# Low parts of the normed input on GpSimd instead of VectorE, in seven of the kernel's normalisations

## What is computed

```
def rms_norm(x, g):
    y = x * rsqrt(mean(x * x, axis=-1) + 1e-6)
    return y * g
...
u = rms_norm(h, norm_mix_g[l]);  h = h + mixer_sublayer(u, ...)
h = h + conv_ffn(rms_norm(h, norm_ffn_g[l]), w_up[l], ...)
# conv_ffn: (silu(causal_conv3(h @ w_up's gate half)) * (h @ w_up's value half)) @ w_down
```

## Time and profile before

| | before |
|---|---|
| median of 3 runs | 2057.96 us (2057.04 to 2058.07) |
| the profiled execution's own time | 2058.53 us |
| its span, first to last instruction | 2056.7 us |
| TensorE busy, weight load busy | 2043.4 us, 1925.8 us |
| VectorE busy | 1704.2 us (83%) |
| ScalarE busy | 1104.8 us (54%) |
| GpSimd busy | 289.1 us (14%), 197 instructions |

### The profile page before, as it was taken

The page is one execution under the profiler, slowest core; times in us unless marked ns, Lnnn a source line. Parts: engine busy times, 40 slices in busy tenths (PEclk is TensorE's granted clock), DMA queues, the critical chain, the costliest instruction groups (busy, mean ns, idle before and its releaser), DMA issues.

```text
span 2056.7 us, 35431 instructions
## 1 busy us (share of the span) xinstructions
PE 2043.4 (99%) x14722; PEld 1925.8 (94%) x14722; DVE 1704.2 (83%) x2507; ACT 1104.8 (54%) x1428; POOL 289.1 (14%) x197
## 2 busy tenths in 40 slices
PE   9999999999999999999999999999999999999998
PEld 9999999899999989979989999899988999989897
DVE  8988899888789988898996669777798996758875
ACT  6887366457756635355455445535346445445542
POOL 0212055000004500001201001510000300000430
PEclk9999999999999999999999999999999999999999
DMA  7563555554235465544555444555554554535543
GB/s 267 196 194 142 185 182 185 186 208 144 103 145 183 160 212 198 184 163 148 202 185 185 164 145 184 180 169 208 184 175 150 185 186 183 185 127 182 186 166 119
DMA packets 58287, 361.74 MB, mean 176 GB/s; under 512 B 6736, under 2 KB 9360, under 8 KB 21136
## 3 DMA queue, kind: packets, MB, share of 16 engines
q1 hardware_dynamic: 58128, 359.48, 49.5%
HBM read 358.37 MB, written 1.08 MB: 175 GB/s over the span
## 4 chain that ended last, share of the span: by engine, by line
PE 87%; DVE 7%; issue 2%; ACT 2%; POOL 1%; DMA 0%; SPq 0%; DVEq 0%; ACTq 0%; POOLq 0%
PE acc L651 47%; PE acc L675 11%; PE acc L658 8%; PE acc L650 7%; PE acc L665 4%; DVE w_lo L1226 2%; ACT w_hi L2217 1%; DVE arena L1720 1%; PE acc L795 1%; PE acc L796 1%; PE acc L797 1%; DVE arena L1466 1%; PE acc L1001 1%; DVE arena L1717 1%; PE pA L1050 1%
## 5 line engine op out<-in xcount | busy, mean ns | idle before, releaser
L651 PE MATMUL acc<-in_both,w_hi 128*128 128x256 f32 x6000 | 1092.9, 285 | 1.8 <-issue 0.7
L651 PE MATMUL acc<-in_both,w_lo 128*128 128x256 f32 x3952 | 947.0, 283 | 0.1
L651 PEld LDWEIGHTS acc<-in_both,w_hi 128*128 128x128 f32 x6000 | 936.9, 192 | 6.8 <-issue 3.3
L1226 DVE TENSOR_TENSOR w_lo<-raw,w_hi 128x2048 fp32r<-128x2048 f32 (+1 forms) x349 | 757.0, 2171 | 127.7 <-ACT w_hi L2217 127.1
L2217 ACT CAST w_hi<-raw 128x2048 fp32r<-128x2048 f32 (+1 forms) x349 | 630.4, 1808 | 229.7 <-PE acc L651 143.8
L651 PEld LDWEIGHTS acc<-in_both,w_lo 128*128 128x128 f32 x3952 | 695.5, 192 | 4.5 <-DVE w_lo L1612 0.3
L2934 POOL TENSOR_TENSOR in_both<-arena,in_both 128x256 fp32r<-128x256 f32 (+1 forms) x112 | 159.4, 1423 | 1145.1 <-ACT in_both L2786 509.1
L675 PE MATMUL acc<-in_both,w_hi 128*128 128x512 f32 x952 | 227.9, 391 | 0.0
L675 PEld LDWEIGHTS acc<-in_both,w_hi 128*128 128x128 f32 x952 | 175.4, 188 | 34.2
L1998 DVE SCALAR_TENSOR_TENSOR arena<-arena,cols 128x256 f32<-128x256 f32 x480 | 200.7, 493 | 0.0
L658 PE MATMUL acc<-in_both,w_hi 128*128 128x512 f32 x704 | 168.9, 391 | 2.2 <-DVE arena L1720 1.4
(11 more groups left out here) (314 smaller groups left out, 1831.0 us busy)
## 6 DMA issues: line engine op xcount, KB each, us to landing
raw<-in_wide SPq DMA_DIRECT2D x285, 1024.0 KB, 4.8
raw<-in_narrow SPq DMA_DIRECT2D x64, 704.0 KB, 4.0
arena<-cs_rows SPq DMA_DIRECT2D x16, 256.0 KB, 4.7
arena<-in_mem SPq DMA_DIRECT2D x3, 1024.0 KB, 6.9
x<-in_x SPq DMA_DIRECT2D x4, 256.0 KB, 6.6
raw<-in_wide SPq DMA_DIRECT2D x2, 512.0 KB, 5.8
tables<-in_tables SPq DMA_DIRECT2D x1, 1024.0 KB, 17.2
arena<-cs_rows SPq DMA_DIRECT2D x16, 64.0 KB, 5.4
```

The source lines that it names most:

```text
L651: return mm(outs[m], w[:, k, at], moving[:, c, :], start=start, stop=stop)
L1226: tt(w_lo[g % RAW][:, 0:n], raw[g % RAW][:, 0:n], w_hi[g % HI][:, 0:n], ALU.subtract).then_inc(lo_ready, 1)
```

## The change

In `norm`, VectorE doesn't make the four low parts any more. GpSimd makes them, with the same four subtractions of 128x512, at the head of its program for the stage, each as soon as ScalarE has the high part of the piece. The Mamba norm, the attention's second norm and the low parts of the memory and of the convolution branch stay with VectorE.

```
 def norm(name, nth, chunk0=0):
-    seg, half = take.next(), NORM_PIECES // 2
+    seg = take.next()
     split(2, seg, 2)
     reciprocal_std(rstd[:])
     scaled(name, x, rstd, xn, val_ready)
     scale_unit(seg, nth, 0)
-    low_parts(xn, chunk0, half, DC // NORM_PIECES)
     scale_unit(seg, nth, 1)
     split(3, seg, 3)
-    low_parts(xn, chunk0, NORM_PIECES, DC // NORM_PIECES, first=half)
+    E.passed(inh_ready, NORM_PIECES)
...
# in GpSimd's program
+def norm_low_parts(first_piece, chunk0):
+    each = DC // NORM_PIECES
+    for n in range(NORM_PIECES):
+        pool.wait_ge(inh_ready, first_piece + n + 1)
+        d = slots(chunk0 + n * each, each)
+        tt(in_lo[:, d, :], xn[:, n * each:(n + 1) * each, :], in_hi[:, d, :], ALU.subtract).then_inc(in_ready, 1)
...
 def ffn(name, n):          # run()
+    norm_low_parts(piece["norm"][n + 1 if name == "up_a" else 2 * n], 0)
     low_parts(name, piece["hid"][n], ...)
 def mixer(l):              # run()
+    norm_low_parts(piece["norm"][3 + 2 * l], MIXER_AT)
     skip("glu", "ret_q", "ret_k", "ret_v")
+def attention():
+    norm_low_parts(piece["norms"][0], DC)
+    skip("att_k", "att_v", "att_q", "att_o")
```

More of the change, by code:

```diff
@@ L2990, in mamba @@
                 skip("xbc", "z", "ssm_out")
-            stages(mamba, ffn("up_a", 0), lambda: skip("att_k", "att_v", "att_q", "att_o"),
+            def attention():
+                norm_low_parts(piece["norms"][0], DC)
+                skip("att_k", "att_v", "att_q", "att_o")
+            stages(mamba, ffn("up_a", 0), attention,
                    ffn("up_a", 1), second=lambda l: (mixer(l), lambda: skip("mem_q", "mem_v", "mem_o"),
```

## The result

| | before | after |
|---|---|---|
| median of 4 runs each, in turns on one chip | 2058.02 us (2057.04 to 2058.38) | 2071.68 us (2070.78 to 2073.63) |
| ratio | | 1.0069 [1.0056, 1.0081] |
| the profiled execution's own time, its span | 2058.53, 2056.7 us | 2071.14, 2069.3 us |

The kernel became 0.7% slower; 2070.5 us had been forecast, with a range of 2062 to 2075.5. The spans differ by 12.6 us, against 12.5 in the sum; the medians differ by 13.7.

A forecast was written before the change was run, and what follows sets the result against it. TensorE, busy 99% of the span, bounds the kernel. Net delays of 3.14 us (`ffn_a`), 4.15 (`ffn_b`) and 5.18 (attention, mixers) make 12.5 us in all, so a median of 2070.5 us, range 2062 to 2075.5.

The forecast's parts named there:

- GpSimd gets in at the next boundary of a row of back-to-back instructions: In each norm's eight `scaled`, a waiting GpSimd subtraction enters between two VectorE instructions; three holds, 3.15 us.
- rival 2: In each norm, back-to-back `scaled` keep GpSimd out, so the kernel isn't slower: 2055.8 us; chance 0.13.
- One hold, 1.05 us: In each norm, a GpSimd subtraction delays a VectorE instruction with two SBUF inputs by 1.05 us, bounds nothing to 1.30.
- The fourth piece comes ahead of the split: At each norm's end, GpSimd's last piece holds the split of unit 3 for 0.8 us; VectorE 1.57 us later.
- rival 1: In each norm, the split of unit 3 goes before GpSimd's last piece and isn't held: 2064.7 us; chance 0.12.
- Seven new waits at unit 3: After each norm, TensorE waits for the late split of unit 3, by 1.51 to 2.48 us.
- What unit 8 gives back: In the feed-forward layers, unit 8's old waits on VectorE (2.2 us) partly absorb the new lateness: `ffn_b` 0.4 us each.
- rival 3: Dearer: longer holds, attention's room used up, or TensorE's speed suffering behind pauses over 2 us: 2074 to 2077 us; chance 0.10.
- Attention's room: In the attention, before ScalarE's next cast behind its rotary copies, some 0.4 us are left to absorb lateness.

The follow-up runs named there:

- memset kernel: Changed kernel, but the seven norms' low parts are left out and GpSimd fills their places with zeros, reading nothing: 2055.3 us (0.9985 to the kernel before).
- PSUM kernel: Changed kernel, but VectorE first copies 1/std into PSUM and the eight `scaled` read it there; GpSimd's subtractions unchanged: 2055.16 us (0.9986 to the kernel before).
- later piece 3: Changed kernel, but GpSimd's fourth piece waits for VectorE's split of unit 3: 2065.42 us (1.0034 to the kernel before).
- VectorE late: Kernel before, VectorE making all low parts ahead of the split of unit 3, the first piece three times; GpSimd idle at norms: 2072.84 us (1.0072).
- one subtraction: Changed kernel, GpSimd's four subtractions joined into one of 128x2048, begun when all high parts are there: 2075.0 us (1.0085 to the kernel before).
- three norms: Changed kernel, with the change kept only in the attention and two mixers; the four feed-forward norms as before: 2062.93 us (1.0025 to the kernel before).

## Why the prediction held, point by point

**GpSimd gets in at the next boundary of a row of back-to-back instructions (against rival 2): right.** Three of eight `scaled` are held, as the text put it, and the first kernels show from both sides that it is a hold: without GpSimd's reads, and without one of VectorE's SBUF inputs, it is gone. By the Trainium skill (SBUF — State Buffer, "Who interferes with whom"), a GpSimd instruction that only writes doesn't contend with a VectorE instruction of two SBUF inputs, and a VectorE instruction with at most one SBUF input doesn't contend with GpSimd at all outside the two-port modes; the memset kernel's 3.25 us and the PSUM kernel's 3.22 us agree with both.

**One hold, 1.05 us: a little too large.** 6.38 less 3.26 is 3.12, so 1.04 each.

**The fourth piece comes ahead of the split (against rival 1): right.** The split was held for 0.77; forecast 0.8. VectorE enters the stage's work 10.48 after the first `scaled` (254.14 less 243.66), 1.51 later than before; forecast 1.57 (its terms add up to between 1.55 and 1.58).

**Seven new waits at unit 3: right in place, each about 0.1 us too large.** Unit 3 starts at 10.65 to 10.67 in all seven, against 10.77: 0.07 from the holds, 0.04 from the handover, for which I took the 0.14 of the earlier trace rows and which is 0.10 here. The pauses are 1.40 and 2.18 us in the two `ffn_a`, 1.51 in the attention, 1.85 and 1.50 in the mixers, 2.38 and 2.36 in the `ffn_b`: 13.2 us, against 13.9.

**What unit 8 gives back: mis-sized.** 1.5 us were forecast. From the starts of matmuls, TensorE's gaps before unit 8 fell from 0.63 and 1.12 to 0.37 and 0.36 in the `ffn_a`, and from 0.55 to nothing in each `ffn_b`: 2.1 us. So the sum by its own terms should have been 13.2 - 2.1 = 11.1. Half of what is missing is in the two `ffn_b`, where the list of waits gave 0.4 for a gap of 0.55. The other half is in the first `ffn_a`, where the prediction had VectorE without spare time between the norm and unit 8. It had some. GpSimd and VectorE there, before and then after:

```profile
272.26 2.99 POOL L2934 TENSOR_TENSOR in_both<-arena,in_both 128x256 fp32r<-128x256 f32 x1 [0.52 <-ACT in_both L2545]
...
272.36 2.29 DVE L1226 TENSOR_TENSOR w_lo<-raw,w_hi 128x2048 fp32r<-128x2048 f32 x1
275.35 0.88 DVE L1717 TENSOR_SCALAR arena<-acc,cols 128x256 f32<-128x256 f32 x2 [0.71 <-POOL in_both L2934]
```

```profile
273.61 0.74 POOL L2933 TENSOR_TENSOR in_both<-arena,in_both 128x256 fp32r<-128x256 f32 x1 [0.52 <-ACT in_both L2544]
...
273.73 2.78 DVE L1226 TENSOR_TENSOR w_lo<-raw,w_hi 128x2048 fp32r<-128x2048 f32 x1
```

Before, a split held a GpSimd subtraction that takes 0.74 elsewhere, and VectorE then stood idle for 0.71 us until it was done. After, that subtraction came 0.1 us ahead of the split and held it instead (2.78 for 2.29), and VectorE had nothing to wait for: its lateness fell from 1.50 to 1.20 us.

**The clock, which the sum left out: 1.5 us in this execution.** Only rival 3 named TensorE's speed behind pauses of over 2 us. In the profiled execution of the changed kernel it happened once, at the last norm. Windows of TensorE there, after (columns as above):

```profile
1888.00:1892.00 4.00, 1.80 (x9) 1.79 (x9) 3.93 (x5) 2.04 (x3) 0.00 (x0) 0.78 0.65 238
1892.00:1896.00 4.00, 4.00 (x29) 4.00 (x28) 3.93 (x6) 1.89 (x3) 0.75 (x1) 0.79 0.06 25
1896.00:1900.00 4.00, 4.00 (x36) 4.00 (x35) 3.78 (x5) 1.63 (x4) 0.41 (x1) 1.00 0.26 66
```

And the matmuls behind that pause of 2.36 us, TensorE's timeline, after:

```profile
1890.24 0.53 PE L651 MATMUL acc<-in_both,w_hi 128*128 128x256 f32 x1 [2.20 <-issue]
...
1891.00 0.41 PE L651 MATMUL acc<-in_both,w_lo 128*128 128x256 f32 x1
1891.21 0.41 PE L651 MATMUL acc<-in_both,w_hi 128*128 128x256 f32 x1
```

They follow each other at 0.21 us instead of 0.12, with the granted clock at 0.5 (1.2 GHz) from 1890.27 to 1893.68, for 3.41 us: sixteen matmuls, some 0.095 us more for each, 1.5 us. 11.1 and 1.5 make the 12.6 of the spans. The forecast of 12.5 is therefore right in its mechanism, and so close by luck: two errors cancel, 1.4 us too much in the waits and what is given back, and 1.5 us for a mechanism that had only a rival's share. A pause of about 0.3 us at the beginning of the first `ffn_b`, ahead of L1313, stands in the trace after and in those of four experiments: VectorE begins that line 0.46 us after the one before it, and I haven't found why. Against it stand 0.37 us less at the last matmuls of the kernel. All other traces but the memset kernel's have them too, so they belong to the profiled execution of before.

**Attention's room, some 0.4 us:** it took nothing in the changed kernel, and 0.68 us in the one with the later piece 3.

**What stays open.** The PSUM kernel's span is 3.5 us below that of before, while the waits of the earlier trace rows come to 2.2. By the starts of matmuls the gaps at unit 8 came to 2.85 us before, and 2.8 of the 3.5 went there; 0.37 are the last matmuls just named. Some 0.4 us remain unplaced. Why TensorE fell to the low clock behind one long pause and not behind another as long can't be told from these traces.

## What to carry to other kernels

Before moving an elementwise operation from VectorE to GpSimd, count VectorE's instructions with two SBUF inputs that it will meet: each GpSimd instruction that reads SBUF stops the one that it meets for what is left of its own length (1.04 of 1.30 us here, 4.31 of 4.62 for the long one). That was 4 x 0.60 us saved against 3 x 1.04 + 0.77 us lost in each norm, and the price falls due at the next operand that had less slack than that (0.4 to 1.4 us here). If the move is wanted, put one input of VectorE's instructions into PSUM, or let GpSimd only write; a later start or one large piece only moved the hold here, and letting the split go first took back less than half of the loss. Look for holds in the durations of VectorE's instructions, since its busy time counts them as work.

## What the runs showed that I hadn't expected

**Short stretches of low clock behind long pauses.** The trace after and three others have stretches of 3.41 us at 1.2 GHz, each where TensorE comes back from a pause of over 2 us, each worth some 1.5 us:

| kernel | pauses over 2.1 us | stretches at 1.2 GHz |
|---|---|---|
| after | 2.18, 2.38, 2.36 | one, behind the 2.36 |
| VectorE late | 2.15, 2.32, 2.32 | one, behind a 2.32 |
| one subtraction | up to 2.64 | two, behind 2.13 and 2.64 |
| piece 3 later, PSUM, memset, three norms | none (longest 1.83) | none |

The kernel in which GpSimd begins later, where TensorE pauses within unit 3 for up to 2.25 us, has one too, behind a pause of that length. A pause of 2.38 us passed without one, and one of 2.13 didn't, so length alone doesn't decide. Executions scatter more where such pauses are: 2.9 us in the changed kernel, 0.9 where piece 3 is later, 0.6 in the memset kernel. The slower executions of the changed kernel also have the lower mean clock: 0.998 at 2070.78 and 2071.14 us, 0.997 at 2072.21, 0.996 at 2073.63. So the profiled execution, with its one stretch, is among the faster ones, and the median of 2071.68 us probably holds more of this cost than the 1.5 us, but only that execution has a trace.

**The hold is paid by whoever comes second, in both directions.** In the kernel in which GpSimd begins later, four pieces of 1.30 us take 9.13. At the first `ffn_a` of the kernel before, a split makes GpSimd's 0.74 us subtraction take 2.99. An engine that was to be relieved can turn into one that delays its helper by more than it saves.
